# Local heads' scores from rounded high and low parts in a two-block transformer kernel on one core

## The reference, cut to what matters

```python
proj = jnp.einsum('bsd,de->bse', rmsnorm(x, attn_norm_g), w_in)
qa, ka, va, qb, kb, vb, f_logit = jnp.split(proj, IN_SPLITS, axis=-1)
qa, ka = rmsnorm(qa by heads, q_norm_a), rmsnorm(ka by heads, k_norm_a)
# local heads: blocks of 128 queries against their own and the previous block of keys
scores = jnp.einsum('bnqkgd,bnskd->bnkgqs', qb, kb).astype(jnp.float32) * scale
scores = jnp.where(valid, scores + alibi, -jnp.inf)
m = jnp.maximum(jnp.max(scores, axis=-1, keepdims=True), sink)
p = jnp.exp(scores - m)
p = p / (jnp.sum(p, axis=-1, keepdims=True) + jnp.exp(sink - m))
out = jnp.einsum('bnkgqs,bnskd->bnqkgd', p, vb)
```

## Time and profile before

| what | value |
|---|---|
| median of three runs | 2717.94 us (2716.56 to 2718.74) |
| the profiled execution, its own time | 2717.62 us |
| its span, first to last instruction | 2715.7 us |
| TensorE busy | 2628.5 us, 97% |
| VectorE busy | 1837.8 us |
| ScalarE busy | 1326.4 us |
| GpSimd busy | 404.9 us |
| mean granted clock of TensorE | 0.994 of 2.4 GHz |

### The profile page before, as it was taken

The page is one execution under the profiler, slowest core; times in us unless marked ns, Lnnn a source line. Parts: engine busy times, 40 slices in busy tenths (PEclk is TensorE's granted clock), DMA queues, the critical chain, the costliest instruction groups (busy, mean ns, idle before and its releaser), DMA issues. The chain is left out here.

```text
span 2715.7 us, 37071 instructions
## 1 busy us (share of the span) xinstructions
PE 2628.5 (97%) x13612; PEld 2188.7 (81%) x13612; DVE 1837.8 (68%) x2469; ACT 1326.4 (49%) x1952; POOL 404.9 (15%) x359
## 2 busy tenths in 40 slices
PE   8999999999999899999999999989999999999999
PEld 7888876777788888888888788778887888888887
DVE  5761465457534788888888867666635875857878
ACT  3111243567432477877787422455533552525353
POOL 0222212100230122222221112300020000000000
PEclk9999999999999999999999999999999999999999
DMA  3215123411452699999999432100032616253441
GB/s 125 55 49 179 42 76 121 136 37 55 133 184 104 233 375 380 389 380 371 373 371 363 141 105 64 43 1 1 1 132 75 265 48 247 71 187 130 158 183 62
DMA packets 142456, 437.83 MB, mean 161 GB/s; under 512 B 23408, under 2 KB 45680, under 8 KB 110576
## 3 DMA queue, kind: packets, MB, share of 16 engines
q1 hardware_dynamic: 125312, 402.40, 41.2%
q0 software_dynamic: 10656, 20.99, 2.2%
q10 hardware_dynamic: 6352, 12.58, 1.2%
HBM read 387.68 MB, written 66.06 MB: 167 GB/s over the span
## 5 line engine op out<-in xcount | busy, mean ns | idle before, releaser
L2670 DVE TENSOR_TENSOR w_lo<-w_raw,w_hi 128x2048 fp32r<-128x2048 f32 x192 | 437.1, 2294 | 60.3 <-ACT w_hi L2604 59.4
L2604 ACT ACTIVATE w_hi<-w_raw 128x2048 fp32r<-128x2048 f32 x187 | 355.9, 1925 | 39.2 <-PE banks L2731 39.2
L3651 PE MATMUL banks<-b_parts,a_parts 128*128 128x512 f32 x1344 | 306.9, 390 | 6.4 <-DVE a_parts L3706 6.4
L3651 PE MATMUL banks<-a_parts,b_parts 128*128 128x512 f32 x1344 | 306.0, 389 | 2.3 <-DVE a_parts L3706 1.2
L3651 PEld LDWEIGHTS banks<-b_parts,a_parts 128*128 128x128 f32 x1344 | 251.8, 188 | 61.0 <-DVE a_parts L3706 8.9
L3651 PEld LDWEIGHTS banks<-a_parts,b_parts 128*128 128x128 f32 x1344 | 252.0, 188 | 55.2 <-DVE a_parts L3706 1.6
L3680 ACT ACTIVATE b_parts<-w_quarter 128x1024 fp32r<-128x1024 f32 x112 | 118.6, 1059 | 281.4 <-PE banks L3651 266.7
L766 POOL TENSOR_TENSOR w_lo<-w_raw,w_hi 128x512 fp32r<-128x512 f32 (+2 forms) x128 | 153.1, 1201 | 508.8 <-ACT w_hi L745 507.6
L745 ACT ACTIVATE w_hi<-w_raw 128x512 fp32r<-128x512 f32 (+2 forms) x128 | 71.7, 569 | 319.9 <-PE banks L828 300.1
L3700 DVE TENSOR_TENSOR b_parts<-w_quarter,b_parts 128x1024 fp32r<-128x1024 f32 x112 | 136.9, 1223 | 132.5 <-ACT b_parts L3680 132.5
L828 PE MATMUL banks<-w_hi,act_hi 128*128 128x512 f32 (+1 forms) x576 | 219.1, 380 | 3.3 <-issue 2.1
(11 more groups left out here) (546 smaller groups left out, 5560.5 us busy)
## 6 DMA issues: line engine op xcount, KB each, us to landing
w_raw<-in_w SPq DMA_DIRECT2D x192, 1024.0 KB, 7.4
a_parts<-scratch_x_parts SPq DMA_DIRECT2D x42, 1024.0 KB, 4.8
w_raw<-in_w_in SPq DMA_DIRECT2D x80, 256.0 KB, 2.7
w_quarter<-in_w_up SPq DMA_DIRECT2D x16, 1024.0 KB, 6.9
w_quarter<-in_w_down SPq DMA_DIRECT2D x16, 1024.0 KB, 7.8
scratch_x_parts<-a_parts SPq DMA_DIRECT2D x14, 1024.0 KB, 5.1
scratch_gateT<-gate_staged SPq DMA_DIRECT2D x32, 256.0 KB, 2.2
gate<-scratch_gateT SPq DMA_DIRECT2D x32, 256.0 KB, 3.7
```

What stands on the lines that cost most here:

```text
L2604: act.activation(hi[c % SLOTS][:, :], raw[c % TILES][:, :], ACT.Copy).then_inc(hi_done, 1)
L2670: dve.tensor_tensor(lo[c % SLOTS][:, :], raw[c % TILES][:, :], hi[c % SLOTS][:, :].bitcast(F32), ALU.subtract).then_inc(lo_done, 1)
L3651: mm = pe.matmul(out, left, right, start=(start and n == 0), stop=(stop and n == 2))
```

## The change

The local heads' scores are made from high and low parts. In each half of the partitions `qaT[g]` now holds the rounded queries of its heads, and in the other half their low parts instead of zeros. `ka_hi[g]` holds the rounded keys of key head g in both halves, in three slots of 128 tokens that are used in turn; `ka_lo[g]` the low part in one half and zeros in the other. A head's scores are two rounded products, queries x `ka_hi` and queries x `ka_lo`.

Step 2 is now the local queries alone (bank 0), and a new step 3 the local keys alone (bank 1). VectorE makes two subtractions in either. GpSimd fills the other halves in step 3 (`pool_keys`): a memset and two copies for odd tiles, a memset and seven copies for even ones, one after the other; the last of the seven waits for VectorE's subtraction. The steps stand at other units, and after a preparation the next turning waits for ScalarE and VectorE only (`wait_banks_read`); the scores alone wait for GpSimd.

```diff
-    SEQUENCE = [(0, 2), (0, 0), (0, 1), (1, 0), (1, 1), (1, 2)] + [(t, step) for t in range(2, NT) for step in range(3)]
-    OF_ACT, OF_DVE = (2, 2, AKV + 1), (2, 2, 0)
+    SEQUENCE = [(0, 2), (0, 3), (0, 0), (0, 1), (1, 0), (1, 1), (1, 2), (1, 3)] + [(t, step) for t in range(2, NT) for step in (0, 1, 3, 2)]
+    BANKS_OF = ((0, 1), (0, 1), (0,), (1,))
+    OF_ACT, OF_DVE, OF_POOL = (2, 2, 2, 2), (2, 2, 2, 2), ((2, 2, 0, 8), (2, 2, 0, 3))
...
+    def pool_keys(self, pool, t):
+        n, done, k = self.own_slot(t), self.pool_upto[t, 3] - self.OF_POOL[t % 2][3], self.ka_hi
+        copies = [(k[0][self.BOTTOM, n, :], k[0][self.TOP, n, :]), (k[1][self.TOP, n, :], k[1][self.BOTTOM, n, :])]
+        if t % 2 == 0:
+            for r in (self.TOP, self.BOTTOM):
+                copies += [(k[0][r, 0, :], k[0][self.TOP, n, :]), (k[1][r, 0, :], k[1][self.BOTTOM, n, :])]
+            copies.append((self.ka_lo[0][self.TOP, 0, :], self.ka_lo[0][self.TOP, n, :]))
+        pool.wait_ge(self.prep_act, self.act_upto[t, 3])
+        if done:
+            pool.wait_ge(self.prep_pool, done)
+        pool.memset(self.ka_lo[1][self.TOP, t, :].bitcast(F32), 0.0).then_inc(self.prep_pool, 1)
+        done += 1
+        for i, (dst, src) in enumerate(copies):
+            pool.wait_ge(self.prep_pool, done + i)
+            if i == 6:
+                pool.wait_ge(self.prep_dve, self.dve_upto[t, 3])
+            pool.tensor_copy(dst, src.bitcast(F32)).then_inc(self.prep_pool, 1)
...
+    def dve_local(self, dve, t, step, banks):
+        bank, n = banks[step - 2], self.own_slot(t)
+        for g, (own, other) in enumerate(((self.TOP, self.BOTTOM), (self.BOTTOM, self.TOP))):
+            dve.wait_ge(self.prep_act, self.act_upto[t, step] - 1 + g)
+            if step == 2:
+                lo, hi, src = self.v.qaT[g][other, :, :], self.v.qaT[g][own, :, :], self.blocks(bank, own)
+            else:
+                lo, hi, src = self.ka_lo[g][own, (n, t)[g], :], self.ka_hi[g][own, n, :], bank[own, 0:P]
+            dve.tensor_tensor(lo, src, hi.bitcast(F32), ALU.subtract).then_inc(self.prep_dve, 1)
...
+    def wait_banks_read(self, pe, t, step):
+        pe.wait_ge(self.prep_act, self.act_upto[t, step])
+        pe.wait_ge(self.prep_dve, self.dve_upto[t, step])
...
-                27: [turn_first(0, 2, EARLY, (heads["kva"].scaled, NT))],
-                30: [turn_first(0, 0, EARLY, (ops.columns_set, 1), (ops.prep_act, ops.act_upto[0, 2]))],
+                27: [turn_first(0, 2, EARLY, (heads["kva"].scaled, NT)), turn_first(0, 3, EARLY)],
+                30: [turn_first(0, 0, EARLY, (ops.columns_set, 1), *after_both(0, 3))],
...
-    for n, (t, step) in ((30, (0, 2)), (33, (0, 0)), (35, (0, 1)), (37, (1, 0)), (39, (1, 1))):
+    for n, (t, step) in ((30, (0, 2)), (30, (0, 3)), (33, (0, 0)), (35, (0, 1)), (37, (1, 0)), (39, (1, 1))):
...
-        if step < 2:
+        if step != 2:
             pool_steps.setdefault(n, []).append(both_copied(t, step))
...
-        for g, r in enumerate((slice(HD, P), slice(0, HD))):
-            done(dve.memset(v.qaT[g][r, :, :], 0.0))
+        done(dve.memset(ops.ka_lo[0][ops.BOTTOM, :, :].bitcast(F32), 0.0))
...
         scale(3, "kb", range(4))
+        ops.dve_part(dve, 0, 2, EARLY)
+        ops.dve_part(dve, 0, 3, EARLY)
         ops.dve_part(dve, 0, 0, EARLY)
...
-    at_unit = {windows_at[1] - 3: (1, 2)}
+    at_unit = {windows_at[1] - 3: (1, 2), windows_at[1] - 2: (1, 3)}
     for t in range(2, NT):
-        before = min(7, starts[t] - starts[t - 1])
-        for step, p in enumerate((starts[t] - before, starts[t] - before // 2 + before // 7 - before // 6, windows_at[t] - 3)):
+        queries, keys = (4, 2) if t == 2 else (5, 3) if t < 5 else (7, 3)
+        for step, p in ((0, starts[t] - queries), (1, starts[t] - keys), (3, starts[t] - 1), (2, windows_at[t] - (2 if t < 4 else 3))):
             at_unit[p] = (t, step)
...
                 if p == windows_at[u.i]:
-                    ops.wait_prepared(pe, u.i, 2)
+                    ops.wait_prepared(pe, *ops.local_ready(u.i))
...
-                        mm = pe.matmul(pair[:, a * u.keys:(a + 1) * u.keys], qaT[u.g][:, a, :], kaT[:, (u.i + 1) * P - u.keys:(u.i + 1) * P],
-                                       start=True, stop=True)
+                        own = pair[:, a * u.keys:(a + 1) * u.keys]
+                        pe.matmul(own, qaT[u.g][:, a, :], ops.ka_hi[u.g][:, keys, :], start=True, stop=False)
+                        mm = pe.matmul(own, qaT[u.g][:, a, :], lows, start=False, stop=True)
...
                     if in_banks:
-                        ops.wait_prepared(pe, *in_banks)
+                        ops.wait_banks_read(pe, *in_banks)
```

More of the change, by code:

```diff
@@ L2863, in __init__ @@
         self.q_both = [at(f"qb_both{i}", o + 8 * i + 4, [P, BH, P], F32R) for i in range(2)]
-        self.kaT = at("kaT", o + 20, [P, S])
+        self.ka_hi = [at(f"ka_hi{g}", o + 20 + 1.5 * g, [P, 3, P], F32R) for g in range(AKV)]
+        self.ka_lo = [at("ka_lo0", CONST + 4.5, [P, 3, P], F32R), at("ka_lo1", FREE + 16, [P, NT, KVF_W], F32R)[:, :, 0:P]]
         self.c_hi = at("c_hi", CONST + 4, [P, NT, BH], F32R)
@@ L2894, in act_part @@
             else:
-                moves = ((self.kaT[:, self.tile(t)].rearrange("p (a t) -> p a t", t=P), bank[:, 0:P], slice(0, P)),)
+                n = self.own_slot(t)
+                moves = tuple((self.ka_hi[g][r, n:n + 1, :], bank[:, 0:P], r) for g, r in enumerate((self.TOP, self.BOTTOM)))
             for dst, src, r in moves:
                 act.activation(dst, self.blocks(src, r), ACT.Copy).then_inc(self.prep_act, 1)
+    def pool_keys(self, pool, t):
[15 more added lines that the diff above has]
+            pool.tensor_copy(dst, src.bitcast(F32)).then_inc(self.prep_pool, 1)
     def pool_part(self, pool, t, step):
+        if step == 3:
+            return self.pool_keys(pool, t)
         for b in range(2):
@@ L2907, in pool_part @@
             pool.tensor_copy(dst, src.bitcast(F32)).then_inc(self.prep_pool, 1)
+    def dve_local(self, dve, t, step, banks):
[7 more added lines that the diff above has]
+            dve.tensor_tensor(lo, src, hi.bitcast(F32), ALU.subtract).then_inc(self.prep_dve, 1)
     def dve_part(self, dve, t, step, banks):
-        for b, bank in enumerate(banks if step < 2 else ()):
+        if step >= 2:
+            return self.dve_local(dve, t, step, banks)
+        for b, bank in enumerate(banks):
             heads = slice(4 * b, 4 * b + 4)
@@ L3051, in f @@
                 pe.wait_ge(s, count)
-            for b, bank in enumerate(banks):
-                ops.turn_part(pe, t, step, b, bank)
+            for b in ops.BANKS_OF[step]:
+                ops.turn_part(pe, t, step, b, banks[b])
         return f
@@ L3206, in attention2_stage @@
     ops = v.ops
[L3207 removed]
+    k_hi, k_both, q_hi, q_both = ops.k_hi, ops.k_both, ops.q_hi, ops.q_both
     probs, aT = at("probs", RINGS, [P, 3, S]), at("probsT", RINGS + 12, [P, 2, S])
@@ L3289, in _ @@
         def _(pool):
[L3290 to L3293, removed]
+            for t, step in ops.SEQUENCE[7:]:
+                if step == 2:
+                    continue
+                if step < 2:
+                    pool.wait_ge(scored, starts[t - 1])
+                ops.pool_part(pool, t, step)
         @block.vector
@@ L3363, in prepare @@
             def prepare(t, step, after):
-                pe.wait_ge(low_read, after + 1)
-                ops.turn_part(pe, t, step, 0, LOW)
-                if high_upto[after + 1]:
-                    pe.wait_ge(high_read, high_upto[after + 1])
-                ops.turn_part(pe, t, step, 1, HIGH)
+                if 0 in ops.BANKS_OF[step]:
+                    pe.wait_ge(low_read, after + 1)
+                    ops.turn_part(pe, t, step, 0, LOW)
+                if 1 in ops.BANKS_OF[step]:
+                    if high_upto[after + 1]:
+                        pe.wait_ge(high_read, high_upto[after + 1])
+                    ops.turn_part(pe, t, step, 1, HIGH)
             def scores(p):
```

34 lines of the change are left out of this document (21 added, 13 removed).

## The result

The changed kernel takes 2733.06 us (median of six runs, 2724.89 to 2736.42), the kernel before 2718.34 us beside it (six runs, 2716.56 to 2721.22). The ratio is 1.0051, 95% interval 1.0041 to 1.0061: slower by 0.5%, 14.7 us. Forecast were 2718.5 us and no measurable change, 2710 to 2724.5 as the range. The profiled execution took 2732.82 us, 2731.1 us of it the span, 15.4 us more than before's span.

The account below looks back on a forecast made before the run. TensorE was taken to bound the kernel (97% busy), the softmax chain the attention's first 29 us. Attention -2.4 plus projection +3.1 gave +0.7, so 2718.5 us and no measurable change; range 2710 to 2724.5.

Parts of the forecast that it names:

- the keys' transpose as a step of its own: Last unit of the tile before: TensorE waits for VectorE's copy of HIGH, 4 x 2.0 = +8.0 us for tiles 4 to 7.
- Products: Attention's window units: eight rounded products in 0.94 us instead of 1.79, 0.85 us back in 12 units, -10.2 us.
- the whole attention: Sum of products, keys' transposes, other moves and bank waits from 1741 to 1985 us: -2.4 us.
- Tile 2's keys' transpose: Attention: old step 2 already waited there for the same copy; its query transposes turn on VectorE's own time, nothing lost.
- tile 3's: Keys' transpose in the attention: the same copy was already waited for, query transposes (0.44 us) move away, +0.5 us.
- The wait behind it for ScalarE's keys: Turning after step 3: ScalarE first ends the window unit's exponentials, then copies; 0.6 us in tile 5, 0.3 in tile 6.
- The projection: Its end: TensorE waits until VectorE has read both local banks, then for GpSimd; +3.1 us, between 1.6 and 5.0.
- VectorE's scaling: Projection: eight passes of 0.69 us without stretch end at 1711.8, or 1713.3 if GpSimd's copies stop VectorE.
- six small copies of GpSimd: Projection, between VectorE's scaling passes: each might stop VectorE for its own 0.25 us.
- The softmax chain takes the gain: Rival, attention: window units run at the VectorE and ScalarE chain's pace, shorter scores pay nothing; 2728.5 us, chance 0.13.
- The gain stays: Rival, attention: shorter scores pay in full, later slack takes up step 3's stops; 2711 us, or 2709.5; chance 0.22.

Follow-up runs that it names:

- The fills: Changed kernel with eight thrown-away full-precision identity products ahead of the keys' transpose at the last unit of tiles 1 to 6: 2721.20 us, ratio 1.0006.
- the combined kernel: Changed kernel with local keys of tiles 2 to 7 turned beside the local queries, and VectorE's local parts ahead of the projection's key scaling: 2709.14 us, ratio 0.9967.

## Why the prediction was wrong

**The step that failed** is the price of the keys' transpose as a step of its own, 4 x 2.0 = +8.0 us, and the sentence that it rests on, that the granted clock is 1.00 "in spite of the idle time in it". The stops came as forecast: 1.89, 1.82, 1.84 and 1.87 us in tiles 4 to 7, 7.4 us against 8.0. What the clock does behind them was put at nothing. But idle time of 0.9 us in 30, in pieces of 0.17 to 0.47, is no evidence for a single piece of 1.9 us; the longest piece that left the clock at 1.00 in that kernel's attention was 1.38 us. The clock loss behind the stops was 11.96 us, 10.25 of it behind those four. The fills gave back 11.9 us of the median, and the four stops put into the old kernel cost 15 instead of 7.4.

**What was right or off by little.** Products: each of the eight went at 0.12 us and the unit held TensorE for 1.04 us, 0.75 less than before (forecast 0.85). With the stops gone, the rest of the attention behind tile 1 takes 216.6 us in place of 226.07, 9.5 us less, beside a forecast of 10.2 for the products alone. In the changed kernel the whole attention, without the clock loss behind the stops, is at -1.0 us (-1.7 and +0.7 for its first part); forecast was -2.4. Tile 2's keys' transpose was put at nothing and tile 3's at +0.5; both stopped for 2.01 and 1.84 us, where before the same copy was waited for 0.92 and 0.71 us. So the stop came in all six tiles. The wait behind it for ScalarE's keys, forecast at 0.6 us in tile 5, was 0.52.

**The projection** was put at 3.1 and measured 2.6 us. TensorE stopped 1.38 us (forecast 2.5) and then 0.63 for GpSimd (0.65). The way between the two marks grew by 2.6 us, 1.55 up to the turned queries, 0.93 from there to the next turning and 0.15 at the end. The mis-sized part is VectorE's scaling. Its timeline in the changed kernel:

```profile
1709.40 0.78 DVE L902 TENSOR_TENSOR kb_aug<-kb_aug,kb_r 128x512 f32<-128x512 f32 x1
1710.21 0.69 DVE L903 TENSOR_TENSOR kb_aug<-kb_aug,gains 128x512 f32<-128x512 f32 x1
...
1713.79 1.41 DVE L2949 TENSOR_TENSOR qaT<-banks,qaT 64x512 fp32r<-64x512 f32 x2
```

The eight passes ran from 1708.07 to 1713.79, 5.7 us, where I had added 1.5 us to 5.52 for six small copies of GpSimd. The copies did not stop VectorE for their own length. It was GpSimd that waited, as its own timeline there shows (the six as one row, then the fourth of them by itself, then the lone seventh):

```profile
1708.51 3.98 POOL L2927 CAST ka_hi<-ka_hi 64x128 fp32r<-64x128 f32 x6
...
1710.39 0.67 POOL L2927 CAST ka_hi<-ka_hi 64x128 fp32r<-64x128 f32 x1
...
1715.97 0.29 POOL L2927 CAST ka_lo<-ka_lo 64x128 fp32r<-64x128 f32 x1 [3.48 <-DVE ka_lo L2949]
```

The six take 0.40 to 0.67 us each, 0.61 on average, where the lone one takes 0.29. The Trainium skill, page "SBUF — State Buffer", section "Who interferes with whom", adds to the rule that the prediction drew on that the order of issue decides who waits. The trace agrees: the last five copies each begin when one of VectorE's passes has begun 0.2 to 0.3 us earlier and end some 0.15 us after that pass has ended (the fourth at 1711.06, the pass of 1710.21 at 1710.90), while the passes themselves took 0.69 to 0.78 us.

**The rivals.** "The softmax chain takes the gain" had the right sign and a sum 4.6 us short (2728.5 us), but not for its reason, so that was luck: where the stops were taken away, the shorter scores paid. "The gain stays" is what the combined kernel does (2709.14 us against the 2709.5 worked out for it), but it is another program, which removes the stops that this rival had to explain away. That the numbers agree so closely is luck too: its attention is 8.6 us shorter than before, not 9.9, and its projection 0.2 us longer, not 1.6. No rival had the clock in it. Once a stop of 2 us was on the list, its rate afterwards had to be an item with a bound, and the earlier trace rows had a row for one: the only window there with 0.94, tile 0's, is also the one with gaps of 0.4 to 1.4 us.

## What to carry to other kernels

A stop of TensorE is to be priced twice, by its length and by what the clock does behind it; the second can be the larger, here 10.3 us on 7.4 for the four stops of tiles 4 to 7. So a new wait in a stretch where TensorE is all but full is worth moving to a unit where the bank has long been read, before anything else is tuned. If it can't be moved, some thrown-away products in it are a cheap cure, and in an experiment they are the edit that tells the clock's part from the wait's. Where another engine sets the pace, as in tile 0, the cure gave nothing here; whether the half clock itself costs anything there was not parted from the cost of the fills.

## What the runs showed of the hardware

- Stops of 1.82 to 2.01 us in a stretch that is otherwise at 1.00 were followed by 3 to 10 us at 0.5 of the clock in seven of ten cases (four of six in the changed kernel, three of four in the old one with stops). Chance alone hardly picks them: in all four profiles of kernels that keep the six stops (the changed one, those with the third product, with the local parts first, and with full products in tile 0) the clock fell after the same four, for the keys of tiles 2, 5, 6 and 7, and not after those of tiles 3 and 4. In the old kernel with stops it was tile 5's that was spared. What spares a stop the rows don't show.
- Shorter stops can do it too: where the weighing was moved ahead, the clock halved at one of 1.10 us and one of 1.62 us, and in the old kernel with stops once behind a wait of 1.08 us. Others of 1.02 to 1.47 us behind tile 0, in these and the other profiles, left it whole, so the rows give no length that is safe.
- In tile 0 the drop began 3.1 us after the attention's first product in the changed kernel and 9.2 us after it in the kernel before; the other profiles with the changed kernel's tile 0 have it at 2.0 to 4.7 us. Fuller products moved it to 6.6 and 10.7 us, a third rounded product to 7.1, filled gaps removed it: the gaps have a part in it, the work between them seems to have one (one profile for each form), and their shares stay open.
- A GpSimd copy of 64x128 took 0.29 us alone and 0.63 to 0.67 when it began behind a VectorE pass of 0.69 us; the passes grew to 0.78 at most.
- Ten executions of kernels with the same code up to tile 0's local keys' transpose differ by up to 5.9 us in when they reach it (1703.14 to 1709.03 us), so marks inside a stage told the parts of this change apart better than the spans did.
